# Gate matmuls of a block-diagonal recurrence: own tile plus a gathered tile in place of neighbouring tiles

## What is computed

```python
LRU_WIDTH = 1280
LRU_BLOCKS = 16
LRU_BW = LRU_WIDTH // LRU_BLOCKS        # 80

def rg_lru(x_c, conv_w, conv_b, w_a, b_a, w_x, b_x, lam):
    ...
    xb = xc.reshape(B, S, LRU_BLOCKS, LRU_BW)
    r = jax.nn.sigmoid(jnp.einsum('bshi,hij->bshj', xb, w_a).reshape(B, S, C) + b_a)
    i = jax.nn.sigmoid(jnp.einsum('bshi,hij->bshj', xb, w_x).reshape(B, S, C) + b_x)
    log_a = -LRU_C * rf * jax.nn.softplus(-lam.astype(jnp.float32))
    a = jnp.exp(log_a)
    mult = jnp.sqrt(jnp.maximum(1.0 - jnp.exp(2.0 * log_a), 0.0))
    bterm = mult * (i.astype(jnp.float32) * xc.astype(jnp.float32))
    ...
    _, h = lax.associative_scan(combine, (a, bterm), axis=1)
```

## Time and profile before

| | |
|---|---|
| median of 3 runs | 3190.51 us (3189.75 to 3190.66) |
| the profiled execution: its time | 3190.44 us |
| its span | 3189.1 us |
| TensorE busy | 3169.5 us, 99% |
| VectorE (DVE) busy | 1835.7 us, 58% |
| ScalarE (ACT) busy | 1243.9 us, 39% |
| stage of the change, layer 2 | 2115.4 to 2259.8 us |
| stage of the change, layer 3 | 2897.6 to 3042.0 us |

### The profile page before, as it was taken

How to read it: one execution, slowest core, us unless ns; L and a number is a source line. 1 busy time by engine, 2 the same in 40 slices (tenths; PEclk the granted TensorE clock), 3 DMA queues, 4 the chain that set the end, 5 groups by cost and what they waited for, 6 DMA issues and landing times.

```text
span 3189.1 us, 37007 instructions
## 1 busy us (share of the span) xinstructions
PE 3169.5 (99%) x14964; PEld 2654.6 (83%) x14964; DVE 1835.7 (58%) x2469; ACT 1243.9 (39%) x1866; POOL 396.0 (12%) x293
## 2 busy tenths in 40 slices
PE   8999999999999999999999999999999999999999
PEld 7888888888888888888888888888888888888887
DVE  6875456665687545656557543447545754345744
ACT  3332334344333233434445422236534442224642
POOL 0201212210020121211011000110012000011001
PEclk9999999999999999999999999999999999999999
DMA  4322223235442222323532222222232132222222
GB/s 167 116 99 93 99 93 112 94 132 188 139 125 93 99 93 100 106 97 119 194 125 78 97 99 87 97 86 98 97 122 87 67 104 94 86 99 95 92 94 101
DMA packets 100232, 339.71 MB, mean 107 GB/s; under 512 B 12288, under 2 KB 12544, under 8 KB 99296
## 3 DMA queue, kind: packets, MB, share of 16 engines
q1 hardware_dynamic: 96736, 322.76, 29.8%
q0 software_dynamic: 3184, 14.06, 1.3%
q10 hardware_dynamic: 144, 0.52, 0.1%
HBM read 326.29 MB, written 2.10 MB: 103 GB/s over the span
## 4 chain that ended last, share of the span: by engine, by line
PE 97%; DVE 1%; issue 1%; ACT 0%; DMA 0%; POOL 0%; POOLq 0%
PE ps L500 96%; PE ps L605 1%; PE ps L844 0%; DVE r L1427 0%; DVE wl L1417 0%; DMA X<-x_in 0%; POOL sm L2020 0%; ACT f L1265 0%; DVE h L1560 0%; DVE sm L1853 0%; PE ps L555 0%; DVE f L1553 0%; DVE f L1803 0%; DVE f L1863 0%; DVE r L1835 0%
## 5 line engine op out<-in xcount | busy, mean ns | idle before, releaser
L500 PE MATMUL ps<-h,wh 128*128 128x512 f32 (+1 forms) x5824 | 1702.5, 376 | 2.2 <-DVE h L1560 1.8
L500 PEld LDWEIGHTS ps<-h,wh 128*128 128x128 f32 x5824 | 1066.8, 189 | 199.3 <-issue 4.6
L500 PE MATMUL ps<-h,wl 128*128 128x512 f32 (+1 forms) x2912 | 1093.2, 375 | 0.0
L1417 DVE TENSOR_TENSOR wl<-raw,wh 128x1024 fp32r<-128x1024 f32 (+3 forms) x596 | 751.8, 1272 | 319.6 <-ACT wh L957 318.7
L957 ACT CAST wh<-raw 128x1024 fp32r<-128x1024 f32 (+3 forms) x596 | 595.9, 1008 | 720.1 <-PE ps L500 718.3
L500 PEld LDWEIGHTS ps<-h,wl 128*128 128x128 f32 x2912 | 548.7, 188 | 98.8
L500 PE MATMUL ps<-r,wh 128*128 128x512 f32 x1632 | 503.8, 390 | 0.0
L500 PEld LDWEIGHTS ps<-r,wh 128*128 128x128 f32 x1632 | 305.2, 188 | 62.7
L500 PE MATMUL ps<-r,wl 128*128 128x512 f32 x816 | 317.5, 389 | 0.0
L1032 ACT CAST r<-f 128x512 fp32r<-128x512 f32 x186 | 114.6, 620 | 511.9 <-DVE f L1756 148.5
L500 PE MATMUL ps<-wh,r 128*128 128x512 f32 x960 | 302.6, 390 | 0.3
(11 more groups left out here) (152 smaller groups left out, 2085.9 us busy)
## 6 DMA issues: line engine op xcount, KB each, us to landing
raw<-wst SPq DMA_DIRECT2D x544, 512.0 KB, 3.3
raw<-wst SPq DMA_DIRECT2D x48, 320.0 KB, 2.8
f<-gains POOLq DMA_DIRECT2D x6, 1024.0 KB, 5.2
raw<-wst SPq DMA_DIRECT2D x16, 384.0 KB, 3.0
f<-f SPq DMA_DIRECT2D x72, 64.0 KB, 2.0
f<-tab POOLq DMA_DIRECT2D x16, 256.0 KB, 5.0
r<-r SPq DMA_DIRECT2D x32, 128.0 KB, 2.3
X<-x_in SPq DMA_DIRECT2D x4, 512.0 KB, 8.4
```

The costliest lines, as they stand in the source:

```text
L500: return e.matmul(o, a, b, start=start, stop=stop, skip_group_check=True)
L1417: e.tensor_tensor(l[:, 0:WIDTH[c]], raw[:, c % NRAW, 0:WIDTH[c]], h[:, 0:WIDTH[c]].bitcast(F32), ALU.subtract).then_inc(*lo_cut.up(("lo", c)))
```

## The change

Each gate multiplies the tile's own channels (3 passes), and then one tile `far` into which SP has copied the needed channels of other tiles (`FAR` lists, for each t = j mod 5, distance, first row and number of rows). Where these are 32 (t = 0, 2, 4: `stacked`), the copy is made four times, as high, low, high, low part on 32 partitions each, the weights are laid out as high, high, low, low parts on the same partitions, and one pass does all products; where they are 128 (t = 1, 3), high and low copies are two tiles and the passes three. DVE cuts the stacked chunks with three instructions in place of one. Every `lru` chunk has 512 columns. SP issues the copies (`far`) in front of the chunk with number 10 + t of the half, after its wait for that chunk's buffer; they are 4, 4, 8, 4, 4 transfers of 16 to 64 rows for t = 0 to 4. TensorE waits for them between own and far passes.

```diff
+FAR = (((1, 0, 32),), ((-1, 64, 64), (1, 0, 64)), ((-1, 112, 16), (1, 0, 16)), ((-1, 64, 64), (1, 0, 64)), ((-1, 96, 32),))
+def stacked(j):
+    return j % 5 % 2 == 0
...
-                out.append((f"{L}/lru{j}", [(w, l, i, j, "lru") for w in ("lru_w_a_2", "lru_w_x_2")
-                                            for i in lru_tiles(j)]))
+                out.append((f"{L}/lru{j}", [(w, l, kind, j, "lru") for w in ("lru_w_a_2", "lru_w_x_2")
+                                            for kind in ("own", "far")]))
...
+FAR_AT = {NAME[f"{_L}/xc{_j - _j % 5}"] + 10 + _j % 5: (_L, _j) for _L in (2, 3) for _j in range(10)}
...
-                        ks = lru_tiles(j)
-                        xc = [(R(21 + k - 5 * hf), R(26 + k - 5 * hf)) for k in ks]
+                        t = j % 5
                         h, l = weights(f"{L}/lru{j}")
-                        for k in ks:
-                            w.wait_ge(*at("xc_lo", L, k))
-                        o = take(("ra", L, j))
-                        group(o, h, l, [k * P for k in range(len(ks))], xc).then_inc(
-                            *group_done.up(("done", ("ra", L, j))))
-                        o = take(("ri", L, j))
-                        group(o, h, l, [(len(ks) + k) * P for k in range(len(ks))], xc).then_inc(
-                            *group_done.up(("done", ("ri", L, j)), ("closed", NAME[f"{L}/lru{j}"])))
+                        w.wait_ge(*at("xc_lo", L, j))
+                        for c, key in ((0, "ra"), (2 * P, "ri")):
+                            own, far = slice(c, c + P), slice(c + P, c + 2 * P)
+                            o = take((key, L, j))
+                            three(o, h[:, own], l[:, own], R(21 + t), R(26 + t), True, False)
+                            w.wait_ge(*at("far", L, j))
+                            if stacked(j):
+                                last = mm(o, l[:, far], R(37 + t), False, True)
+                            else:
+                                last = three(o, h[:, far], l[:, far], R(37 + t), R(47 + t), False, True)
...
+                    if c in STACKED:
+                        l, f, h = (a[:, 0:4 * P].rearrange("p (g k c) -> p g k c", g=2, k=2) for a in (
+                            l, raw[:, c % NRAW, :], h.bitcast(F32)))
+                        e.tensor_tensor(l[:, :, 0, :], f[:, :, 0, :], h[:, :, 0, :], ALU.subtract)
+                        e.tensor_tensor(l[64:P, :, 1, :], f[64:P, :, 1, :], h[64:P, :, 1, :], ALU.subtract)
+                        e.tensor_copy(l[0:64, :, 1, :], h[0:64, :, 1, :]).then_inc(*lo_cut.up(("lo", c)))
+                        continue
...
+            def far(L, j):
+                t = j % 5
+                for d, r, n in FAR[t]:
+                    w.wait_ge(*at("xc_lo", L, j + d))
+                times, tall = (4, 32) if stacked(j) else (2, 0)
+                for g in range(times):
+                    dst, row = R(37 + t + (0 if stacked(j) else 10 * g)), tall * g
+                    for d, r, n in FAR[t]:
+                        last = (g, d) == (times - 1, FAR[t][-1][0])
+                        e.dma_start(dst[row:row + n, :].bitcast(F32), R((21, 26)[g % 2] + t + d)[r:r + n, :].bitcast(F32)).then_inc(
+                            *far_done[t].up(*((("far", L, j),) if last else ())))
+                        row += n
...
             for c in range(len(CHUNKS)):
                 if c >= NRAW:
                     w.wait_ge(*at("lo", c - NRAW))
+                if c in FAR_AT:
+                    far(*FAR_AT[c])
```

More of the change, by code:

```diff
@@ L32, in rng @@
     return (a, a + n)
-def lru_tiles(j):
-    b0, b1 = (j * P) // 80, (j * P + P - 1) // 80
-    return list(range((b0 * 80) // P, (b1 * 80 + 79) // P + 1))
+FAR = (((1, 0, 32),), ((-1, 64, 64), (1, 0, 64)), ((-1, 112, 16), (1, 0, 16)), ((-1, 64, 64), (1, 0, 64)), ((-1, 96, 32),))
+def stacked(j):
+    return j % 5 % 2 == 0
 WO = [(c, n) for c in range(4) for n in range(2)]
@@ L349 @@
 SPREAD_AT = {NAME[f"{_L}/q0"] + _n: (_L, _r) for _L in (0, 1) for _r, _n in ((0, 12), (2, 14))}
+STACKED = {NAME[f"{_L}/lru{_j}"] for _L in (2, 3) for _j in range(10) if stacked(_j)}
+FAR_AT = {NAME[f"{_L}/xc{_j - _j % 5}"] + 10 + _j % 5: (_L, _j) for _L in (2, 3) for _j in range(10)}
 SWAP_AT = {}
@@ L465, in build @@
         spread_done = {r: Signal(sem(f"s_spread{r}"), 16) for r in (0, 2)}
-        signals += swap_done + list(spread_done.values())
+        far_done = [Signal(sem(f"s_far{t}"), 16) for t in range(5)]
+        signals += swap_done + list(spread_done.values()) + far_done
         loads = {}
@@ L916, in mixer2 @@
                     for j in range(5 * hf, 5 * hf + 5):
-                        ks = lru_tiles(j)
-                        xc = [(R(21 + k - 5 * hf), R(26 + k - 5 * hf)) for k in ks]
+                        t = j % 5
                         h, l = weights(f"{L}/lru{j}")
-                        for k in ks:
-                            w.wait_ge(*at("xc_lo", L, k))
-                        o = take(("ra", L, j))
-                        group(o, h, l, [k * P for k in range(len(ks))], xc).then_inc(
-                            *group_done.up(("done", ("ra", L, j))))
-                        o = take(("ri", L, j))
-                        group(o, h, l, [(len(ks) + k) * P for k in range(len(ks))], xc).then_inc(
-                            *group_done.up(("done", ("ri", L, j)), ("closed", NAME[f"{L}/lru{j}"])))
+                        w.wait_ge(*at("xc_lo", L, j))
[8 more added lines that the diff above has]
+                                last = three(o, h[:, far], l[:, far], R(37 + t), R(47 + t), False, True)
+                            closes = (("closed", NAME[f"{L}/lru{j}"]),) if key == "ri" else ()
+                            last.then_inc(*group_done.up(("done", (key, L, j)), *closes))
                         tile(f"{L}/zc{j}", xs)
@@ L2240, in pack_weights @@
             if p[4] == "lru":
-                w, l, i, j, _ = p
-                out[n, :, c:c + P] = dense[w][l, i * P:(i + 1) * P, j * P:(j + 1) * P]
+                w, l, kind, j, _ = p
+                of = dense[w][l][:, j * P:(j + 1) * P]
+                rows = [of[j * P:(j + 1) * P]]
+                if kind == "far":
+                    rows = [of[(j + d) * P + r:(j + d) * P + r + m] for d, r, m in FAR[j % 5]] * (4 if stacked(j) else 1)
+                out[n, :, c:c + P] = np.concatenate(rows)
                 c += P
```

## The result

The changed kernel takes 3202.3 us, median of 6 runs (3201.95 to 3204.08), against 3190.33 us before: a ratio of 1.0039, 95% interval 1.0026 to 1.0051. It is slower by 12 us, although it does 120 matmuls less, 27.2 us of TensorE's work. The forecast was 3200.3 us. The profiled execution took 3204.08 us, with a span of 3202.7.

What follows compares the result with a forecast made beforehand. TensorE, busy 3169.5 of 3189.1 us, was taken as the bound. Per layer, waits of 15.65 less 13.6 saved and 0.2 hidden gave +1.9: 3194.3 us; 6.0 for the clock made 3200.3 us, range 3192 to 3207.

Steps and rivals of the forecast that it cites:

- A: TensorE's wait at `lru0` for the first gather, landing at 2147.4 instead of going on at 2143.28: 4.1 us per layer.
- the clock: Half clock for some 3.2 us behind A and behind C: 1.5 us lost each time, 6.0 us in all.
- B: TensorE's wait at `xc9` for DVE's low part, there at 2209.55: 3.0 us per layer.
- C: TensorE's wait at `lru5` for the gather, landing at 2223.2 and wanted at 2215.67: 7.5 us per layer.
- D: TensorE's wait at `prc_0+` for the low part of c's tile 9: 1.05 us per layer.
- the swap: Swap of the rotary tiles, four SP transfers, taken as nearest row for a gather: 4.0 us from SP's turn to reader.
- the loop of ACT and DVE: Closed loop from the tanh of `zc1` that does not shorten; starting 1.9 us late, it ends up +1.35 us.
- the case I gave 0.45: The clock falls after both gather waits, A and C: 3200.3 us, chance 0.45.
- more of the same: Rival: half clock twice as long after each wait, 3206.3 us, chance 0.12.
- the 0.2 us at 2217.57: Cost of an instruction fetch before the change, taken as hidden afterwards: 0.2 us per layer.
- The rival of gathers in time: SP can issue the first gather by 2139.3, so A and C are gone: 3175.6 us, chance 0.09.
- the sentence on the gathers of t = 1 to 4: These later gather waits cost nothing; the tightest, t = 1, landed by 2152.3 and wanted at 2154.8.

Runs made afterwards that it cites:

- the first run with an earlier gather: The changed kernel with the transfers for tiles 0 and 5 issued in front of chunk 8 instead of 10: 3191.65 us.
- the new gate order: The changed kernel with ACT and DVE cutting four chunks ahead in xc and projection c's gate tiles one place earlier: 3173.66 us, ratio 0.9945.
- cuts four ahead: The changed kernel with ACT and DVE cutting four chunks ahead instead of two in the xc tiles: 3177.11 us, ratio 0.9957.
- the filler: The changed kernel with 16 (tile 0) and 31 (tile 5) additional, overwritten TensorE passes during the gather waits: 3196.88 us.

## Why the prediction was right

By its steps, for layer 2, predicted and measured:

| | predicted | measured |
|---|---|---|
| matmuls removed | 120 | 120 |
| A, gather at `lru0` | 4.1 | 3.79 |
| lost to the clock behind A | 1.5 | 2.8 |
| tanh of `zc1` later than before | 1.9+1.5 = 3.4 | 4.56 |
| B, low part of `xc9` | 3.0 | 2.88 |
| SP's turn for tile 5 | 2219.2+1.5 = 2220.7 | 2221.85+0.14 |
| C, gather at `lru5` | 7.5 | 7.21 |
| lost to the clock behind C | 1.5 | 2.8 |
| D, `prc_0+` | 1.05 | 0.92 |
| waits in all | 15.65 | 14.80 |

The waits came out as sized, each within about 0.3 us, as they are sums of durations in fixed orders of other engines; the swap was the right row for the gather (4.0 against 3.85 and 3.91 us). That the loop of ACT and DVE passes lateness on, and cedes what it had idled, is in the row at 2189.66 in the timeline of ACT after the change: the table load ahead of the fifth gates, at 2185.77 before, is 4.0 us late where the tanh of `zc1` was 4.6 late. The three instructions of a stacked cut take 0.42, 0.42 and 0.29 us, starting 1.07 us before what follows, where the one took 0.60 by the same measure: 0.47 more instead of 0.37.

The term that was mis-sized is the clock. I took the one stretch at half clock at the start of the span, 3.1 us, as the length of work at it; behind A and behind C it was 5.7 us (in layer 3 3.4 behind A, 5.7 behind C). Predicted were 3.0 us per layer, measured 5.6 in layer 2 and 4.5 in layer 3, so the clock cost 4.1 us more than I said; the waits, 29.6 us in the two layers instead of 31.3, cost 1.7 less. The span grew by 13.6 us: the last waits of the two layers (2281.30 and 3069.80) lie 788.5 us apart instead of 782.2, so layer 3 added 6.3 and layer 2 7.3. Waits and clock, less the 13.6 saved, give 6.8 and 5.7; the other 0.5 to 0.6 us per layer are in neither and stay open. The profiled execution stands 3.8 and the median 2.0 us above the forecast.

So it is in part luck that the forecast came as near: its two errors have opposite signs. That both gathers would bring the clock down, the case I gave 0.45, is what happened, but three of the four stretches cost 2.8 us, nearly the 3.0 of "more of the same", to which I gave 0.12. And that the clock falls behind waits of 2.0 to 3.0 us too, as in five of the experiments, no case of mine had.

My reading of the start of the span was wrong as well. I took the 1.7 us in which TensorE idled there as a gap that suffices to bring the clock down. But it went back to work at 16.38 at full clock, and the clock fell only at about 17.6, 1.2 us later; what brought it down there no row shows.

```profile
16.00:17.00 1.00, 0.62 (x5) 0.65 (x6) 0.83 (x2) 1.00 (x3) 0.00 (x0) 1.00 0.99 363
```

Nor does a row show that the 0.2 us at 2217.57, which the sum counts, was an instruction fetch: the earlier trace rows has it under "issue", a wait for nothing that the profile shows.

The rival of gathers in time was right in size, 3175.6 against 3176.57 measured without gathers, but wrong in its condition: "SP can issue the first gather by 2139.3" isn't enough, as the first run with an earlier gather showed. The step that failed there is the sentence on the gathers of t = 1 to 4: its margin of 2.5 us was counted on a TensorE made late by A. The same holds for the 6.8 us that it gave the chunk held back by the eight transfers of t = 2: with the gathers early, ACT waited 0.8 us for it.

What is open: how much of the 4.6 us between runs of the kernel with the new gate order is the clock. Its two runs of 3174.9 and 3175.0 us have a mean granted clock of 0.998, the two faster ones 0.999, and 0.001 of the span is 3.2 us; but in the kernel with cuts four ahead the two runs with 0.998 are the faster ones, so a fall does not always show in the time. Only one execution of each kernel has rows that tell where it fell.

## What to carry to other kernels

When one engine is busy all of the time, work taken from it is gained only up to what the next engines' fixed chains allow; add up that chain before counting the passes, and look for other work to put ahead of the point where it is waited for. A transfer placed in an in-order queue starts when the queue gets there and not when its data are ready: read off what the queue waits for at that place, and read the margin of each later transfer again with the first wait taken away. A wait on TensorE costs more than its length when the clock falls behind it; filling it with useless passes was a gain here, and so was useful work put there (the gate tiles of projection c).

## What the runs showed of the hardware

In the profiled executions and the two layers of the change, the granted clock was down behind every wait of TensorE of 3.58 us and more (3.58, 3.79, 3.79, 3.84, 7.13 and 7.21). With waits of 2.87 to 3.27 us it differed: it fell at 2.88 to 2.90 with the first gather earlier and with the filler, but not at 2.87 to 2.90 in the changed kernel and without a gather; it fell at 2.95 and 3.27, but not at 3.01. It fell behind waits of 2.42 and 2.47 us and one of 1.99 us, and not behind two of 2.2, one of 2.30 or any shorter than 1.99. So between 2 and 3.3 us the length of the wait alone does not tell.

A stretch at 1.2 GHz lasted 3.4 us in most cases (also at the start of the span of the kernel before), 6.8 us in three, and 10.2 us at both waits C; part of the long ones lay in the wait itself, and TensorE worked 2.9 to 5.9 us of each. Where it did not begin in the wait, it began up to 1.5 us after TensorE was back at work.

Four transfers within SBUF, of 32 rows and 64 KB each, were with their reader 3.9 us after SP's turn, 2.4 us of it SP's issue.
